# The mixer's output projection of a two-layer block as 2x2 block products, seven of eight for each contraction side

## What is computed

```python
x = x + 0.5 * swiglu_ffn(rms_norm(x, ffn1_norm_g), ffn1_w_in, ffn1_w_out)
proj = rms_norm(x, mix_norm_g) @ w_mix_in
y_rwkv = rwkv7_time_mix(proj[..., :RWKV_PROJ], ...)          # (256, 512)
y_moba = moba_attention(q_m, k_m, v_m, rel_bias)             # (256, 512)
x = x + concatenate([y_rwkv, y_moba], -1) @ w_mix_out        # 1024 x 1024: the part that is changed
x = x + memory_cross_attention(rms_norm(x, xattn_norm_g), ...)
x = x + 0.5 * swiglu_ffn(rms_norm(x, ffn2_norm_g), ffn2_w_in, ffn2_w_out)
```

## Time and profile before

| what | value |
|---|---|
| median of three runs | 2289.99 us (2289.5 to 2291.07) |
| the profiled execution | 2290.4 us, span 2288.6 us |
| granted TensorE clock over the span | 0.998 of full speed |
| TensorE busy / its weight loads | 98% / 67% of the span |
| VectorE / ScalarE / GpSimd busy | 53% / 19% / 2% |

### The profile page before, as it was taken

How to read it: one execution, slowest core, us unless ns; L and a number is a source line. 1 busy time by engine, 2 the same in 40 slices (tenths; PEclk the granted TensorE clock), 3 DMA queues, 4 the chain that set the end, 5 groups by cost and what they waited for, 6 DMA issues and landing times.

```text
span 2288.6 us, 30857 instructions
## 1 busy us (share of the span) xinstructions
PE 2245.7 (98%) x12850; PEld 1544.3 (67%) x12850; DVE 1221.6 (53%) x2256; ACT 429.0 (19%) x864; POOL 53.2 (2%) x77
## 2 busy tenths in 40 slices
PE   7999999999999999999999999999999999999998
PEld 5778854444444358849867778848865976687873
DVE  2798431111111166668663666667666765457675
ACT  1123321111110021101323221102100132222110
POOL 1000100000000010000000000000000000000000
PEclk9999999999999999999999999999999999999999
DMA  9656569999999975434331544526544442245541
GB/s 406 259 225 262 224 200 381 422 422 422 422 422 422 422 236 169 174 139 166 125 125 39 184 145 159 184 92 221 184 158 157 163 147 76 82 140 171 169 173 48
DMA packets 176007, 499.86 MB, mean 218 GB/s; under 512 B 6905, under 2 KB 99337, under 8 KB 146065
## 3 DMA queue, kind: packets, MB, share of 16 engines
q1 hardware_dynamic: 171920, 481.23, 55.8%
q0 software_dynamic: 3824, 16.43, 2.3%
q10 hardware_dynamic: 144, 0.52, 0.1%
HBM read 491.34 MB, written 6.82 MB: 218 GB/s over the span
## 4 chain that ended last, share of the span: by engine, by line
PE 88%; DMA 8%; DVE 2%; ACT 1%; issue 1%; SPq 0%; POOL 0%; POOLq 0%; DVEq 0%
PE bank L2286 22%; PE bank L2334 11%; PE bank L1468 7%; DMA ring<-in_w 7%; PE bank L898 6%; PE bank L2399 6%; PE bank L1505 3%; PE bank L2509 2%; PE bank L2804 2%; PE bank L2875 2%; PE bank L2503 2%; PE bank L2770 2%; PE bank L1452 2%; PE bank L1489 2%; PE bank L888 1%; PE bank L1002 1%
## 5 line engine op out<-in xcount | busy, mean ns | idle before, releaser
L2286 PE MATMUL bank<-Tw,Sx 128*128 128x256 f32 x1032 | 229.9, 379 | 0.0
L2286 PEld LDWEIGHTS bank<-Tw,Sx 128*128 128x128 f32 x1032 | 193.0, 190 | 24.6
L2286 PE MATMUL bank<-ring,xT 128*128 128x256 f32 x688 | 155.8, 379 | 0.3 <-DVE Tw L3220 0.3
L2286 PEld LDWEIGHTS bank<-ring,xT 128*128 128x128 f32 x688 | 130.4, 190 | 18.7 <-DVE Tw L3220 0.7
L898 PE MATMUL bank<-xT,ring 128*128 128x256 f32 x640 | 141.8, 380 | 0.0
L898 PEld LDWEIGHTS bank<-xT,ring 128*128 128x128 f32 x640 | 120.7, 190 | 19.0 <-issue 3.3
L1812 DVE TENSOR_TENSOR sg<-sg,bank 128x512 f32<-128x512 f32 x16 | 11.0, 688 | 202.8 <-PE bank L1468 202.8
L1468 PE MATMUL bank<-ring,xg 128*64 128x512 f32 x512 | 113.9, 593 | 5.3 <-DMA ring<-in_w 5.3
L1505 PE MATMUL bank<-ring,hTg 128*64 128x512 f32 x512 | 113.4, 595 | 0.0
L1468 PE MATMUL bank<-more,xg 128*64 128x512 f32 x512 | 112.6, 592 | 0.0
L3290 DVE TENSOR_TENSOR whole<-bank,part 128x256 f32<-128x256 f32 (+1 forms) x133 | 57.4, 432 | 98.6 <-PE bank L2286 97.5
(11 more groups left out here) (603 smaller groups left out, 3802.0 us busy)
## 6 DMA issues: line engine op xcount, KB each, us to landing
ring<-in_w SPq DMA_DIRECT2D x128, 1024.0 KB, 17.4
ring<-in_ffn_w_in SPq DMA_DIRECT2D x88, 1024.0 KB, 7.6
ring<-in_first_pieces SPq DMA_DIRECT2D x33, 2048.0 KB, 12.0
more<-in_w SPq DMA_DIRECT2D x64, 1024.0 KB, 17.2
ring<-in_ffn_w_out SPq DMA_DIRECT2D x20, 2048.0 KB, 7.9
ring<-in_w_mix_in SPq DMA_DIRECT2D x12, 2048.0 KB, 7.8
ring<-in_xattn_w_kv SPq DMA_DIRECT2D x8, 2048.0 KB, 8.1
ring<-in_w_mix_out SPq DMA_DIRECT2D x4, 2048.0 KB, 10.2
```

Source lines behind the costliest of these rows:

```text
L2286: last = nc.tensor.matmul(bank[BANK_OF[name]][:, 0:SEQ], lhs(k), rhs(k), start=(k == 0), stop=(k == 3))
```

## The change

Both layers' output projections become 2x2 block products. For each contraction side the activations are split in two token halves and two contraction halves (`x11`, `x12`, `x21`, `x22`), the weights in two contraction halves and two column halves. VectorE forms four sums of the activations (`S`, 128x256) and four differences of the weights (`T`, 128x1024) for each side. TensorE makes seven products of two matmuls each, attention's side into seven banks first and the RWKV side on top of it in the same banks. `mixer_residual` combines the seven banks into `x`.

The order changes too. The first half of attention's P1 goes in front of the wait for the copy of the last solve, its second half in front of the means. One matmul of P2 stands between means and squares, and the squares now use the means' banks. The rest of attention's products follow behind the squares. The weight differences and attention's sums are made by VectorE between `masked(13)` and the means. The differences of the query weights are a function, `query_weights`: unit 0 stays where it was, unit 1 moves behind the sums of `cross`. ScalarE copies P1's bank behind its gain and bias. SyncE's queue frees the two slots after P2 and P3. The rest of the diff renames semaphores (`xo_ready` to `out_sums`, `xa_oc` to `out_copied`) and shifts their counts.

```diff
+        MO_BANK = {"P1": 2, "P6": 5, "P7": 4, "P5": 6, "P2": 3, "P4": 0, "P3": 7}
+        def mo_T(side):
+            if side == MOBA:
+                T1, T2, T4 = (t.rearrange("p (k a) t -> p k (a t)", k=2)
+                              for t in (pT[:, 0:4, :], pT[:, 4:8, :], kk[:, :, :]))
...
+            return T1, T2, mo_w(side)[1], T4
...
-                    sp.wait_ge(out_psum, l * N_OUT + (4 + 2 * (j - J_MIXOUT + 1)))
+                    sp.wait_ge(out_psum, mo_done(l, ("P2", "P3")[j - J_MIXOUT]))
...
+            def mixer_out(side, name, ks=(0, 1)):
+                x11, x12, _, x22 = mo_x(side)
+                w11, _, w21, w22 = mo_w(side)
+                S1, S2, S3, S4 = mo_S(side)
+                T1, T2, T3, T4 = mo_T(side)
+                x_, w_ = {"P1": (x11, w11), "P2": (x12, w21), "P3": (S4, w22), "P4": (x22, T4), "P5": (S1, T1),
+                          "P6": (S2, T2), "P7": (S3, T3)}[name]
+                for k in ks:
+                    last = nc.tensor.matmul(bank[MO_BANK[name]][:, :], x_[:, k, :], w_[:, k, :],
+                                            start=(side == MOBA and k == 0), stop=(side == RWKV and k == 1))
+                if side == RWKV:
+                    last.then_inc(out_psum, 1)
...
                 solve(1, bank[7])
+                wait_piece2(pe, J_MIXOUT, l)
+                mixer_out(MOBA, "P1", (0,))
                 pe.wait_ge(u_taken, l * N_U + 8)
...
             def group_norm(l):
+                mixer_out(MOBA, "P1", (1,))
                 for n in range(2):
                     pe.wait_ge(yy_taken, l * 2 + n + 1)
...
-                mixer_out(l, 0, (4, 5, 6, 7))
+                mixer_out(MOBA, "P2", (0,))
                 for n in range(2):
                     pe.wait_ge(gn_sq, l * 2 + (n + 1))
-                    nc.tensor.matmul(bank[2 + n][:, :], K[:, HEADS, :], xs[:, 0, n * 512:(n + 1) * 512],
+                    nc.tensor.matmul(bank[n][:, :], K[:, HEADS, :], xs[:, 0, n * 512:(n + 1) * 512],
                                      start=True, stop=True).then_inc(heads_psum, 1)
-                mixer_out(l, 1, (4, 5, 6, 7))
+                mixer_out(MOBA, "P2", (1,))
+                wait_piece2(pe, J_MIXOUT + 1, l)
+                pe.wait_ge(out_sums, l * N_XO + 1)
+                for name in ("P7", "P6", "P5", "P3"):
+                    mixer_out(MOBA, name)
+                pe.wait_ge(gn_rs, l * 2 + 1)
+                mixer_out(MOBA, "P4")
+
+                pe.wait_ge(ycat, l * 2 + 1)
+                mixer_out(RWKV, "P1")
+                pe.wait_ge(out_sums, l * N_XO + 2)
+                mixer_out(RWKV, "P6")
+                mixer_out(RWKV, "P7")
+                mixer_out(RWKV, "P5")
                 pe.wait_ge(ycat, (l + 1) * 2)
-                mixer_out(l, 0, (0, 1, 2, 3))
-                mixer_out(l, 1, (0, 1, 2, 3))
+                mixer_out(RWKV, "P2")
+                mixer_out(RWKV, "P4")
+                pe.wait_ge(out_sums, l * N_XO + 3)
+                mixer_out(RWKV, "P3")
...
+                act.wait_ge(out_psum, mo_done(l, "P1"))
+                nc.scalar.activation(flat(part[:, 0:2, :]), bank[MO_BANK["P1"]][:, :], ACT.Copy).then_inc(out_copied, 1)
...
                 masked(13)
+                for n in range(2):
+                    wait_piece2(dve, J_MIXOUT + n, l)
...
+                st(minus(B1, u12, u11))
+                st.sync()
+                st(minus(B3, u22, u12))
+                st(minus(B2, u22, B1))
+                dve.wait_ge(u_psum, l * N_U + 6)
+                dve.wait_ge(mb_oc, (l + 1) * 2)
+                st(add(A1, y21, y22))
+                st(minus(A3, y11, y21))
+                st.sync()
+                st(minus(A2, A1, y11))
+                st.sync()
+                st(minus(A4, y12, A2))
+                st.sync()
+                minus(B4, u21, B2).then_inc(out_sums, 1)
...
+                dve.wait_ge(u_psum, l * N_U + 7)
+                st(minus(B1, u12, u11))
+                st.sync()
+                st(minus(B3, u22, u12))
+                st(minus(B2, u22, B1))
+                st.sync()
+                st(minus(B4, u21, B2))
...
                     nc.vector.tensor_tensor(t, t, gT[:, 2 * n:2 * n + 2, :], ALU.mult).then_inc(ycat, 1)
+                    dve.wait_ge(ycat, l * 2 + n + 1)
+                    if n == 0:
+                        st(minus(A3, y11, y21))
+                st(add(A1, y21, y22))
+                st.sync()
+                minus(A2, A1, y11).then_inc(out_sums, 1)
+                dve.wait_ge(out_sums, l * N_XO + 2)
+                minus(A4, y12, A2).then_inc(out_sums, 1)
+                query_weights(l, 0)
-                add_tokens(4, out_psum, l * N_OUT + 4, l * 4 + 5)
+            def mixer_residual(l):
...
+                dve.wait_ge(out_copied, l * N_XA + 1)
+                st(to_x(0, 0, E1))
+                dve.wait_ge(out_psum, mo_done(l, "P6"))
+                st(add(U2, ps["P6"], E1))
+                st.sync()
+                st(to_x(0, 1, U2))
+                dve.wait_ge(out_psum, mo_done(l, "P7"))
+                st(add(U3, ps["P7"], U2))
+                st.sync()
+                st(to_x(1, 0, U3))
+                st(to_x(1, 1, U3))
+                st.sync()
+                dve.wait_ge(out_psum, mo_done(l, "P5"))
+                st(to_x(0, 1, ps["P5"]))
+                st(to_x(1, 1, ps["P5"]))
+                dve.wait_ge(out_psum, mo_done(l, "P2"))
+                st(to_x(0, 0, ps["P2"]))
+                st.sync()
+                dve.wait_ge(out_psum, mo_done(l, "P4"))
+                to_x(1, 0, ps["P4"]).then_inc(x_first, 1)
+                dve.wait_ge(out_psum, mo_done(l, "P3"))
+                to_x(0, 1, ps["P3"]).then_inc(x_ready, 1)
...
                 nc.vector.tensor_tensor(S4, x12, S2, ALU.subtract).then_inc(xq_dve, 1)
+                query_weights(l, 1)
                 dve.wait_ge(rstd_ready, l * 4 + 7)
```

More of the change, by code:

```diff
@@ L1967, in mx_part, with mo_done, mo_x, mo_w @@
             return mx_two(u, t[:, 0:P] if u == 5 else t)
-        N_OUT, N_XO, N_XA = 11, 4, XH + 1
+        N_OUT, N_XO, N_XA = 14, 7, XH + 2
+        MO_BANK = {"P1": 2, "P6": 5, "P7": 4, "P5": 6, "P2": 3, "P4": 0, "P3": 7}
+        MOBA, RWKV = 0, 1
+        def mo_done(l, name):
+            return l * N_OUT + (4 + list(MO_BANK).index(name) + 1)
+        def mo_x(side):
+            c = 4 * (1 - side)
+            return [xT[:, c + 2 * b:c + 2 * b + 2, t * P:(t + 1) * P] for t in range(NT) for b in range(2)]
+        def mo_w(side):
+            c = 4 * (1 - side)
+            halves = [slot_w(slot_of(J_MIXOUT + n), KD, 512) for n in range(2)]
+            return [halves[n][:, c + 2 * b:c + 2 * b + 2, :] for b in range(2) for n in range(2)]
+        def mo_S(side):
+            return [Sx[:, n, 2 * side:2 * side + 2, :] for n in range(4)]
+        def mo_T(side):
+            if side == MOBA:
+                T1, T2, T4 = (t.rearrange("p (k a) t -> p k (a t)", k=2)
+                              for t in (pT[:, 0:4, :], pT[:, 4:8, :], kk[:, :, :]))
+            else:
+                three = Mrk[:, :, :].rearrange("p h n -> p (h n)").rearrange("p (a k n) -> p a k n", a=3, k=2)
+                T1, T2, T4 = (three[:, n, :, :] for n in range(3))
+            return T1, T2, mo_w(side)[1], T4
         XO_BANK = {"P1": 0, "P7": 1, "P2": 4, "P6": 5, "P5": 6, "P4": 7, "P3": 2}
         def xo_done(l, name):
-            return l * N_OUT + (8 + list(XO_BANK).index(name) + 1)
+            return l * N_OUT + (11 + list(XO_BANK).index(name) + 1)
         XQ_PROD = ("P1", "P2", "P6", "P5", "P7", "P3", "P4")
@@ L3115, in mixer @@
                     act.wait_ge(heads_psum, l * N_HEADS + (n + 7))
-                    st(nc.scalar.activation(xs[:, 1, n * 512:(n + 1) * 512], bank[2 + n][:, :], ACT.Ln,
+                    st(nc.scalar.activation(xs[:, 1, n * 512:(n + 1) * 512], bank[n][:, :], ACT.Ln,
                                             scale=1.0 / HD, bias=lnx_eps[:, 0:1]))
@@ L3153, in out @@
                     act.wait_ge(at_o, l * N_AT + (NH + h + 1))
-                    nc.scalar.activation(flat(xT[:, 2 * h:2 * h + 2, :]), bank[h][:, :], ACT.Copy).then_inc(xa_oc, 1)
+                    nc.scalar.activation(flat(xT[:, 2 * h:2 * h + 2, :]), bank[h][:, :], ACT.Copy).then_inc(out_copied, 1)
                 query(0, "E1")
@@ L3175, in cross @@
                         act.wait_ge(out_psum, xo_done(l, "P1"))
-                        nc.scalar.activation(flat(part[:, 0:2, :]), bank[XO_BANK["P1"]][:, :], ACT.Copy).then_inc(xa_oc, 1)
+                        nc.scalar.activation(flat(part[:, 0:2, :]), bank[XO_BANK["P1"]][:, :], ACT.Copy).then_inc(out_copied, 1)
                         out(2)
@@ L3688, in mixer @@
                     nc.vector.tensor_tensor(t, t, gT[:, 2 * n:2 * n + 2, :], ALU.mult).then_inc(ycat, 1)
[L3689 to L3699, removed]
@@ L3700, in mixer, with add, to_x @@
```

(23 more changed lines are left out.)

43 lines of the change are left out of this document (27 added, 16 removed).

## The result

The changed kernel takes 2279.06 us in the median of five runs (2277.78 to 2281.26) beside 2289.99 for the kernel before (2288.16 to 2291.16). The ratio is 0.995, with a 95% interval of 0.9939 to 0.9961: faster by 0.4 to 0.6%. The forecast was 2280.4, with a range from 2278.6. The median lies 0.5 us inside that edge; by the ratio, 0.995 of 2289.99, the time is 2278.5 and lies 0.1 us outside. The direction and the mechanism came as forecast.

What follows compares the result with a forecast made beforehand. TensorE, busy 98% of the span, was taken to bound the kernel. Fewer matmuls and filled idle time were to save 5.0 us in each of two layers, 10.0 from 2290.4: 2280.4 us, range 2278.6 to 2284.4.

Steps and rivals of the forecast that it cites:

- Pace and number of matmuls: TensorE's output products: 28 matmuls instead of 32 at 0.86 us each, saving 3.44 us in a layer.
- The holes: TensorE's waits before the last outputs (0.70 us) and the means (0.26), to be filled by halves of attention's P1.
- The chain: Squares, logarithm, root, gate and sums on ScalarE and VectorE: first gate near 1253.2, last sum 1257.1, no product waiting.
- The tail: VectorE behind the gate: 4.8 us of query weights, then ten adds, 6.75 us up to `x_first`, near 1268.6.
- The stage: Output-projection stage up to the transposes: they start near 1268.6 instead of 1273.63, 5.0 us earlier in each layer.
- The moved query weights: Unit 1's differences behind cross-attention's last sum: hold VectorE 4.8 us, 3 us of slack, so no cost.
- VectorE's tail as the end: VectorE's work behind the gate ends the stage: 2.4 us gained a layer at 0.93 an add; half-way, 2283.6; chance 0.16.
- only the matmuls: In both stages, idle time returns at new waits, leaving 2 x 3.44 = 6.9 us gained: 2283.5; chance 0.14.
- a table load at twice its row: ScalarE's two loads cost 1.28 us more each, `x_first` 2.6 us later: 2.4 gained a layer, 2285.6; chance 0.02.
- The slower rival: VectorE's weight differences and sums fall behind the means: stage 6.4 us later than before in a layer, 2303; chance 0.03.
- the base of the sum: The profiled execution's 2290.4 us, from which 10.0 us for two layers were taken; the runs' median was 0.4 below it.
- both holes and all adds at their best: The better rival, for TensorE's waits and VectorE's adds in the stage: 5.6 us a layer, 2279.2; chance 0.07.

Runs made afterwards that it cites:

- The second five runs: The changed kernel measured once more, nothing altered, against the kernel before: 2280.58 us, ratio 0.9952.
- the two added instructions: The changed kernel with two query-weight differences (128x1024, 1.22 us each) made twice behind the gate, against the kernel before: 2286.34 us, ratio 0.9978.

## Why the prediction was right, and where it was wrong

The mechanism held, step by step. In what follows 1.08 us are taken off the times after, to put them on the old clock.

- *Pace and number of matmuls*: 0.429 us a pass stays (a product of two matmuls every 1.72 us); 56 passes were forecast and 56 stand in each layer's timeline.
- *The holes*: half right. The waits are gone, but half of P1 took 1.06 us in the first hole (1240.84 to 1241.90) and 0.96 in the second, where 0.86 had been taken. Outputs came 0.3 late (0 to 0.16 forecast), means 0.9 (0.6), VectorE's subtraction 0.8 (0.7 was given as the limit of a right forecast). The holes are worth 0.90 us, as emptying them showed.
- *The chain*: the first gate was forecast to start at 1253.2 and started at 1253.21; the last sum was to end at 1257.1 and ended at 1257.05; the weights were to end at 1261.9, and the first add starts at 1261.77. No product waited.
- *The tail*: the adds to `x_first` took 6.57 us, 6.75 had been added up from independent and dependent pairs. `x_first` came at 1268.34 where 1268.6 was forecast; TensorE ended the stage at 1268.55, where 1268.4 was forecast. Which of the two ends it was forecast the other way round, but the time to 0.1 us.
- *The stage*: 5.0 us a layer forecast, 5.08 measured; that adds 0.2 us to the 10.0.
- *The moved query weights* cost nothing: in the changed kernel the queries' products follow the transposes with no idle time.
- *Rivals*: VectorE's tail as the end, only the matmuls, and a table load at twice its row did not happen; the logarithm starts 0.02 us behind its load, also now that nothing hides it. The slower rival was priced too high: carried out, it made the stage 1.7 and 0.7 us longer than before, not 6.4, because VectorE waits 5.21 us for ScalarE's root behind the means (1251.71 in its timeline of the changed kernel), and that much of the moved work fits into it.

**The step that failed** is the base of the sum and the range around it. The sum stood on one execution, 2290.4, and what executions differ in outside the stage was put at nothing, without a reason, though three runs of the kernel before spread over 1.6 us. So the low end, "both holes and all adds at their best, 5.6 in a layer: 2279.2", took in only what was unknown in the stage, and the chances were built on it. The runs showed in its place that executions of one and the same kernel differ by several us: the 45 runs of the kernel before have a median of 2290.71 and a standard deviation of 1.6 us, and that most of what the profiled ones differ in outside the stage is the granted clock of the first block.

From the forecast 2280.4 to the measured 2279.06 there are 1.3 us. Of these, 0.4 is the one execution against the median of its kernel (2290.4 less 2289.99), 0.2 is the stage (10.17 for 10.0), and 0.8 is left, for which nothing in the stage accounts. That the first five runs came out near 2279.2 is luck, as far as these runs can tell, and not the cause that was named for that figure: the stage gained 5.08 us a layer, not 5.6. The second five runs gave 10.1 (2290.71 less 2280.58), all ten against all 45 give 11.25 (2290.71 less 2279.46), and in the experiments above the times and the stages differ by up to 1.3 us to either side. Which execution was favoured by how much cannot be told for the first five, as no clock is known for the runs of the kernel before beside them. The size of the change was right to 0.2 us; a range of the stage's unknowns, widened by some 1.5 us on each side for the executions, would have held the time.

## What to carry to other kernels

Fewer matmuls shorten a stage only as far as the chain on the other engines allows: here seven of eight products gave 0.7 us a layer in the old order and 5.1 together with an order that feeds that chain first and uses TensorE's free work as filler only where it waits. New elementwise work belongs into the time when its engine is idle ahead of the critical chain, and behind the chain it costs its full length once the slack is used up, as the two added instructions showed. For effects of some tenths of a per cent the stage's length in the trace is the better measure, and a predicted time needs the spread of the executions on top of the stage's own bounds.

## What was not expected of the hardware

- A wait of 3.82 us in the middle of a dense stretch was followed by passes at half the granted clock: 12 passes took 7.96 us in one layer and 6.92 in the other, where 5.15 is their time at full clock.
- A single 128x512 matmul between groups of small ones took 1.06 and 0.96 us of TensorE's time instead of 0.86: a filler costs more where it breaks into such groups.
- With TensorE busy all the time, on one core, the granted clock of the first block's window from 96 to 108 us was 0.72, 0.86 or 1.00 in executions of the same program, at 0.50 for some 6 us in one of them. This and a second window (120 to 180 us, 0.97 or 1.00) moved the start of the second block by up to 4 us.
